# Stick-breaking attention steps that score, scale and take the magnitude of a unit one step ahead, with slab evacuations moved to the head of VectorE's step and slab copies behind the logarithm on ScalarE

## The reference

```
proj = rmsnorm(h) @ w_in                      # [1024, 3072]
cb, cc, cu, q, k, v = split(proj)             # six parts of width 512
conv_out = head_rmsnorm(cb * causal_conv3(cc * cu))
for each of 8 heads (width 64), each query i:
    z[j] = q[i] . k[j] / 8
    log_keep[j] = log_sigmoid(-z[j]) for j < i, else 0
    a[j] = exp(log_sigmoid(z[j]) + sum over j' > j of log_keep[j']) for j < i, else 0
    out[i] = sum_j a[j] * v[j]
h = h + concat(conv_out, head_rmsnorm(out)) @ w_out
```

## Time and profile before

| | us |
|---|---|
| median of 3 runs (lowest, highest) | 2588.47 (2588.09, 2589.94) |
| the profiled execution: its time | 2589.27 |
| the profiled execution: its span | 2587.2 |

### The profile page before, as it was taken

The page is one execution under the profiler, slowest core; times in us unless marked ns, Lnnn a source line. Parts: engine busy times, 40 slices in busy tenths (PEclk is TensorE's granted clock), DMA queues, the critical chain, the costliest instruction groups (busy, mean ns, idle before and its releaser), DMA issues.

```text
span 2587.2 us, 33362 instructions
## 1 busy us (share of the span) xinstructions
PE 2525.5 (98%) x12652; PEld 2017.4 (78%) x12652; DVE 1720.6 (67%) x2087; ACT 996.5 (39%) x1431; POOL 1291.2 (50%) x1524
## 2 busy tenths in 40 slices
PE   8999999999999999999999999989999999999997
PEld 7877887687887877877676777768878888888886
DVE  7637773768658568467765555564487877788666
ACT  3627880436315224234465545462211111111132
POOL 4632446535444445353432222224588787887663
PEclk9999999999999999999999999999999999999999
DMA  3111013222112212111320000102232233332512
GB/s 142 50 45 42 17 42 110 69 76 74 66 50 73 66 57 66 66 61 54 131 73 25 25 33 25 33 24 99 82 114 83 89 122 114 122 103 78 212 41 82
DMA packets 53527, 189.90 MB, mean 73 GB/s; under 512 B 5440, under 2 KB 5824, under 8 KB 53376
## 3 DMA queue, kind: packets, MB, share of 16 engines
q1 hardware_dynamic: 31392, 110.11, 12.8%
q10 hardware_dynamic: 21984, 77.73, 8.4%
HBM read 158.33 MB, written 29.49 MB: 73 GB/s over the span
## 4 chain that ended last, share of the span: by engine, by line
PE 85%; DVE 9%; ACT 4%; issue 2%; POOL 0%; ACTq 0%; DVEq 0%; POOLq 0%
PE PS L903 39%; PE PS L1675 10%; PE PS L1649 5%; PE PS L1633 5%; PE PS L1254 4%; PE PS L1160 2%; PE PS L1697 2%; PE PS L1050 2%; PE PS L1081 1%; PE PS L1487 1%; PE PS L1470 1%; PE PS L1066 1%; PE PS L1510 1%; PE PS L1601 1%; PE PS L1287 1%
## 5 line engine op out<-in xcount | busy, mean ns | idle before, releaser
L706 POOL CAST w_hi<-w_stage 128x1024 fp32r<-128x1024 f32 x122 | 148.8, 1220 | 843.5 <-PE PS L903 697.4
L709 POOL TENSOR_TENSOR w_lo<-w_stage,w_hi 128x256 fp32r<-128x256 f32 x488 | 467.2, 989 | 9.8
L903 PE MATMUL PS<-XH,w_hi 128*128 128x512 f32 x1216 | 384.0, 397 | 5.2 <-DVE XL L2813 1.8
L903 PE MATMUL PS<-XL,w_hi 128*128 128x512 f32 x1216 | 375.4, 390 | 0.0
L903 PE MATMUL PS<-XH,w_lo 128*128 128x512 f32 x1216 | 375.1, 390 | 0.0
L903 PEld LDWEIGHTS PS<-XH,w_hi 128*128 128x128 f32 x1216 | 223.2, 188 | 56.2 <-issue 8.3
L903 PEld LDWEIGHTS PS<-XL,w_hi 128*128 128x128 f32 x1216 | 228.4, 188 | 48.7
L903 PEld LDWEIGHTS PS<-XH,w_lo 128*128 128x128 f32 x1216 | 228.3, 188 | 48.4
L806 POOL TENSOR_TENSOR w_lo<-w_stage,w_hi 128x256 fp32r<-128x256 f32 x246 | 205.7, 841 | 0.0
L802 POOL CAST w_hi<-w_stage 128x256 fp32r<-128x256 f32 x246 | 133.3, 545 | 112.1 <-PE PS L903 38.8
L1675 PE MATMUL PS<-ffn_u_hi,w_hi 128*128 128x512 f32 x392 | 152.6, 389 | 0.7 <-DVE H L3358 0.7
(11 more groups left out here) (500 smaller groups left out, 6099.5 us busy)
## 6 DMA issues: line engine op xcount, KB each, us to landing
w_stage<-w SPq DMA_DIRECT2D x202, 512.0 KB, 3.3
H<-h_kept ACTq DMA_DIRECT2D x20, 1024.0 KB, 4.9
ssd_sum_rows<-sums_kept ACTq DMA_DIRECT2D x32, 512.0 KB, 3.6
h_kept<-H ACTq DMA_DIRECT2D x16, 1024.0 KB, 5.0
H<-x_t ACTq DMA_DIRECT2D x8, 512.0 KB, 8.3
pj_kept<-ple_proj_tiles ACTq DMA_DIRECT2D x8, 512.0 KB, 2.6
h_kept<-H ACTq DMA_DIRECT2D x8, 512.0 KB, 3.0
out_t<-out_tiles SPq DMA_DIRECT2D x16, 256.0 KB, 2.1
```

Of the source, the lines that this page charges most:

```text
L706: nc.gpsimd.tensor_copy(w_hi[:, slot, :, :], w_stage[:, slot, :, :]).then_inc(s_w_hi, 1)
L709: nc.gpsimd.tensor_tensor(w_lo[:, slot, k:k + 2, :], w_stage[:, slot, k:k + 2, :], w_hi[:, slot, k:k + 2, :].bitcast(F32), ALU.subtract).t ...
L903: mm = nc.tensor.matmul(outs[:, half, :], wt[:, slot, k, :], a[:, k - first, half * HB:(half + 1) * HB], start=(k == whole[0] and wt is w_ ...
```

## The change

On TensorE, a step now computes the scores of unit s+1 after the early pieces and ahead of the suffix of unit s-1, and the carry of unit s-2 ahead of these scores (in place of the carry of unit s-1 at the step's end). On VectorE, a new helper `sb_scaled` does the scaling of unit s+1 right behind the subtraction of unit s-1, in place of that of unit s at the step's head; and all slab evacuations that belong to the early pieces stand ahead of the subtraction. On ScalarE, `sb_magnitude` takes Abs of unit s+1 at the end of the step (ahead of the root of a head norm), and the slab copies and the head's square stand behind Exp and Ln. Buffers, shapes, the number of instructions and the pieces for each step are the same.

```diff
-        CC_STEPS += _cbs + _taps if (_m, _step) in HEAD_STEPS else _taps + _cbs
+        CC_STEPS += _cbs + _taps
...
                     early, late = SB_FILL[m][step]
-                    if step == 0:
-                        sb_pieces(early)
+                    sb_pieces(early)
+                    if step >= 2:
+                        sb_carry(m, step - 2)
                     if step == 0:
                         sb_scores(m, 0)
-                    else:
-                        sb_pieces(early)
+                    elif step + 1 < NU:
+                        sb_scores(m, step + 1)
                     if 1 <= step <= NU:
                         sb_suffix(m, step - 1)
...
                     sb_pieces(late)
                     if m == 3 and step == NU:
                         out2_tiles(0, range(0, 2))
-                    if step + 1 < NU:
-                        sb_scores(m, step + 1)
-                    if 1 <= step <= NU:
-                        sb_carry(m, step - 1)
+                    if step == 0:
+                        sb_scores(m, 1)
...
+            def sb_magnitude(m, t):
+                q0, T = SB_WIDE[t], NU * m + t
+                act.wait_ge(s_zc, T + 1)
+                nc.scalar.activation(SPF[:, T % 3, :, q0:HB], ZS[:, T % 3, :, q0:HB], ACT.Abs).then_inc(s_al, 1)
...
+                    if step == 0:
+                        sb_magnitude(m, 0)
                     if step < NU:
                         q0, T = SB_WIDE[step], NU * m + step
-                        z, l = ZS[:, T % 3, :, q0:HB], SPF[:, T % 3, :, q0:HB]
-                        act.wait_ge(s_zc, T + 1)
-                        nc.scalar.activation(l, z, ACT.Abs).then_inc(s_al, 1)
+                        l = SPF[:, T % 3, :, q0:HB]
+                    if step < NU:
+                        act.wait_ge(s_al, 3 * T + 1)
+                        nc.scalar.activation(l, l, ACT.Exp, scale=-1.0).then_inc(s_al, 1)
+                        act.wait_ge(s_al, 3 * T + 2)
+                        nc.scalar.activation(l, l, ACT.Ln, bias=1.0).then_inc(s_al, 1)
                     for key in sb_finished(m, step, 0):
                         sb_copies(key)
...
+                    if step + 1 < NU:
+                        sb_magnitude(m, step + 1)
                     if (m, step) in HEAD_STEPS:
                         head_root(HEAD_STEPS[m, step])
...
+            def sb_scaled(m, t):
+                (hf, j), q0, T = SB_UNITS[t], SB_WIDE[t], NU * m + t
+                dve.wait_ge(s_z, T + 1)
+                if T >= 3:
+                    dve.wait_ge(s_o, T - 2)
+                v.scalar_tensor_tensor(out=ZS[:, T % 3, :, q0:HB], in0=PS[:, 0:2, q0:HB], scalar=RK[:, j:j + 1],
+                                       in1=RM[:, hf * HB + q0:(hf + 1) * HB].unsqueeze(1).to_broadcast([P, 2, HB - q0]),
+                                       op0=ALU.mult, op1=ALU.mult).then_inc(s_zc, 1)
...
-                    head_next = (m, step) in HEAD_STEPS
                     for key in sb_finished(m, step, 0):
-                        if head_next:
-                            sb_lows(key)
+                        sb_lows(key)
                     if 1 <= step <= NU:
...
                         v.tensor_tensor(d_, d_, PS[:, 2:4, q1:HB], ALU.subtract).then_inc(s_d, 1)
+                    if step + 1 < NU:
+                        sb_scaled(m, step + 1)
...
-                    for key in sb_finished(m, step, 0):
-                        if not head_next:
-                            sb_lows(key)
```

More of the change, by code:

```diff
@@ L2324, in _ @@
                         head_hi(1)
-                    if step < NU:
-                        act.wait_ge(s_al, 3 * T + 1)
-                        nc.scalar.activation(l, l, ACT.Exp, scale=-1.0).then_inc(s_al, 1)
-                        act.wait_ge(s_al, 3 * T + 2)
-                        nc.scalar.activation(l, l, ACT.Ln, bias=1.0).then_inc(s_al, 1)
                     if 1 <= step <= NU:
@@ L3148, in _ @@
             root_squared()
+            def sb_scaled(m, t):
[6 more added lines that the diff above has]
+                                       op0=ALU.mult, op1=ALU.mult).then_inc(s_zc, 1)
             for m in range(4):
                 for step in range(SB_STEPS):
+                    if step == 0:
+                        sb_scaled(m, 0)
                     if step < NU:
@@ L3153, in _ @@
                         z = ZS[:, T % 3, :, q0:HB]
-                        dve.wait_ge(s_z, T + 1)
-                        if T >= 3:
-                            dve.wait_ge(s_o, T - 2)
-                        hf, j = SB_UNITS[step]
-                        v.scalar_tensor_tensor(out=z, in0=PS[:, 0:2, q0:HB], scalar=RK[:, j:j + 1],
-                                               in1=RM[:, hf * HB + q0:(hf + 1) * HB].unsqueeze(1).to_broadcast([P, 2, HB - q0]),
-                                               op0=ALU.mult, op1=ALU.mult).then_inc(s_zc, 1)
                     if step == 6:
```

## The result

| | before | after |
|---|---|---|
| median of 4 runs (lowest, highest), us | 2588.28 (2588.01, 2589.94) | 2599.84 (2596.56, 2600.92) |
| the profiled execution: time, span, us | 2589.27, 2587.2 | 2599.2, 2597.2 |
| PE's waits, 1322 to 1775 us | 16.5 | 23.5 |

The ratio is 1.0038, with a 95% interval of 1.0026 to 1.005: the change made the kernel slower. The forecast was 2581.0, in a range that ended at 2588.5.

What follows compares the result with a forecast made beforehand. PE was busy 98%, so only its 15.9 us of loop waits and its granted clock could change. Terms summed to -7.7 us: 2581.6 against the profiled execution, 2580.8 against the median, forecast 2581; own range 2577 to 2585, overall 2575 to 2588.5.

Steps and rivals of the forecast that it cites:

- Head sums, -1.7: Step 2 of pairs 1 to 3: the three waits of a head's sum for the evacuation of cb go, -1.7 us.
- Steps 11 and 12 of pairs 0 to 2, -3.0: Evacuation of q leaves the chain, no scaling enters; suffix wait 0.69 and carry's 0.3 go, -1.0 us a pair.
- One scores, one carry, one values.: Claim that the new order leaves TensorE's work between two suffixes the same, so its cover of VectorE's chain stays.
- pair 3 step 11: A tap and one piece: values to suffix goes from 6.80 to 7.39 us, +0.6; suffix wait 2.7 to 3.
- Steps 4 and 6: Pair 0: step 4's suffix wait goes (-2.2 us) with its clock loss (-1.7); step 6's wait for cu goes (-1.6).
- Step 9: Pair 0, tap and two pieces: chain goes from 6.19 to 7.39 us, +1.2; suffix wait 1.5 to 1.7.
- Step 10 of pairs 1 and 2: A tap and three pieces: chain taken as 7.5 us against TensorE's 7.04, +0.45 each.
- The added wait: Scaling of unit s+1 needs unit s-2's value buffer; covered by 0.16 us, so taken as 0.
- rival A: Slower: value-buffer wait or other delay between subtraction and softplus lengthens each full step's chain; +5 us, with clock loss 2595; chance 0.10.
- The clock: Behind the waits that stay (pair 0 step 9, pair 3 step 11), loss bounded by 0 and 1.7 us each, taken as 0.
- rival B: No change to be told: clock falls behind both long waits (+3.4), POOL contention stays in chain (+1.1), 2584.5 us; chance 0.18.

Runs made afterwards that it cites:

- head_early: The changed kernel with the head's sum put between scores and suffix on TensorE and its logarithm ahead of the weights on ScalarE: 2595.29 us, 1.0022 of before.
- gap: Changed kernel with copies and squares first and head's sum early, plus next unit's scaling moved between softplus and low part on VectorE: 2584.38 us, 0.9978 of before.
- q_low_behind: The changed kernel with the low part of q alone put back behind the subtraction on VectorE: 2594.80 us, 1.0021 of before.

## Why the prediction was wrong

**Head sums, -1.7.** This term failed. The three waits for an evacuation did go. The forecast put nothing for what comes behind them. The working looked only at what the sum waits for, not at who waits for the sum's banks: +7.8 in six waits, shown by head_early, which removed 6.2 of them and gained 4.1.

**Steps 11 and 12 of pairs 0 to 2, -3.0.** This term failed too. It moved the evacuation of q ahead of the subtraction and cost it by its own 1.14 us, under TensorE's cover. It did not count that the low part needs ScalarE's copy, which the same change put behind Exp and Ln. Waits of 1.23 + 2.30 + 2.30 = 5.8 came for 3 x 0.69 and the carries' 0.9: +2.9, 5.9 away from the forecast, and 1.7 us of clock behind each wait of 2.30. H and Q with the clock are 7.8 + 5.9 + 3.4 = 17.1 of the 17.6 between the forecast (-7.7) and the profiled execution (+9.9); the clock's second fall in pair 3 adds 1.7 more, and smaller terms of both signs make up the rest. The 3.4 of clock is in part chance, as `head_early` shows.

**"One scores, one carry, one values."** This sentence is wrong at two places. Looking ahead by one moves all scores an interval earlier, so between the suffixes of steps 10 and 11 stands none, and between those of steps 2 and 3 stand the narrow ones of unit 4 for the full ones of unit 3 (the suffix of pair 0 step 3 has a new wait of 0.23). At pair 3 step 11 the chain was 7.38 (1734.22 to 1741.60) as forecast (7.39), but its cover was 0.9 thinner, and the wait 3.79 for a forecast 2.7 to 3.

**Pair 0.** Steps 4 and 6 came as forecast: the suffix of step 4 starts without a wait, at 1349.44 for 1351.04, the clock stays up, the wait for cu is gone. Step 9 waits 2.18 where 1.5 to 1.7 were forecast, as the low part took 1.66 for 1.23 beside POOL. Step 10 of pairs 1 and 2 waits 0.17 for a forecast 0.45.

**The added wait and rival A.** The scaling waited for a value buffer 2.7 us in four times, at most 0.7, and not in the full steps. No suffix waited behind these: the 0 was right, and A's mechanism did not happen. The result lies on A's side for another reason. But the scaling in the chain did cost what the loop's arithmetic says: `gap` takes it out and gains 0.17%.

**The clock, and rival B.** The forecast said that it counted the clock as lost where a row shows it, but it left out the fall behind the 2.24 of pair 3 before, so it took 0 though two of three such waits had lowered the clock. B was partly right: the clock did fall behind the 3.79 (not behind the 2.18 of pair 0). B's own sum is off by one: 2581 + 3.4 + 1.1 is 2585.5, not 2584.5.

So the right method, a serial chain against TensorE's cover, gave near numbers where it was applied. It was applied to the suffix only. Two other waiters, the next piece on the shared banks and the low part of q, had covers of their own that the same move took away.

## What to carry to other kernels

When an in-order engine's work is moved ahead, list what it stood behind, not only what it goes in front of: each move uncovers the release that the moved work was hiding. Check every shared buffer from both sides, who waits for it and what frees it, and every instruction put at the head of a queue for its slowest operand. If one must add work to a serial chain between two engines, the place is where the engine idles for the other inside the chain, here between softplus and low part.

## What the hardware showed

**Clock.** In after the granted clock fell to 0.50 behind waits of 2.30 (1525.39), 2.30 (1642.36), 3.79 and 2.15, and stayed at 1.00 behind 2.18 (1384.26). Before, it fell behind 2.30 and 2.24 and stayed at 1.00 behind 2.31. It stayed at 1.00 behind 1.19 in q_low_behind and behind 2.29 and 2.28 in head_early. So a wait near 2.3 can go either way, and the 0 taken for these in the forecast was one end of a range, not its middle. Each of the six falls before and after lost 1.7 us of full speed. The Trainium skill (TensorE: Matmul & The Clock Gate, Part 1: "The HAM clock gate") has a half and a full level, the full one released by recent activity; the stretches at 0.50 and 1.00 agree with the two levels.

**VectorE beside GpSimd.** The low part of the softplus took 1.66 for 1.23 while POOL ran at pair 0 step 9, the same 0.43 more as the softplus in the earlier trace rows. The low part of q, which has one of its two inputs in PSUM, took 1.22 beside POOL (1519.51, while POOL ran from 1517.67 to 1520.50). The Trainium skill (SBUF — State Buffer, "Who interferes with whom") calls this contention for a shared port an exclusive lock. By that rule a full block by one of the POOL instructions beside it (four in 3.79) would be up to 0.95, an estimate; no row here shows that for the low part.
